# Two products of a high weight joined into one 496-column product: a 4-layer fp32 trunk on one core

## What is computed

```
x += 1/2 * post(SwiGLU_1(pre(x)))         # d_ff = 2816
x += post(Mixer_i(pre(x)))                # layer 0: attention | gated short conv; layer 1: RG-LRU block
x += 1/2 * post(SwiGLU_2(pre(x)))
x += (p[i] @ W_pe) * sigmoid(rmsnorm(x) @ W_pg)
def rmsnorm(x, g): return x * rsqrt(mean(x * x) + EPS) * g
def swiglu(x, wi, wo): g, u = split(x @ wi); return (silu(g) * u) @ wo
```

## Time and profile before

| | |
|---|---|
| median of three runs | 2090.8 us |
| span of the profiled execution | 2089.9 us |
| products and weight loads in it | 17092 each |
| PE busy | 2068.6 us (99%) |
| DVE busy | 1125.9 us (54%) |
| ACT busy | 702.9 us (34%) |
| DMA, mean | 97 GB/s |

### The profile page before, as it was taken

How to read it: one execution, slowest core, us unless ns; L and a number is a source line. 1 busy time by engine, 2 the same in 40 slices (tenths; PEclk the granted TensorE clock), 3 DMA queues, 4 the chain that set the end, 5 groups by cost and what they waited for, 6 DMA issues and landing times.

```text
span 2089.9 us, 37944 instructions
## 1 busy us (share of the span) xinstructions
PE 2068.6 (99%) x17092; PEld 2046.3 (98%) x17092; DVE 1125.9 (54%) x1509; ACT 702.9 (34%) x877; POOL 47.7 (2%) x95
## 2 busy tenths in 40 slices
PE   8999999999999999999999999999999999999999
PEld 8999999999999999999999999999998999999998
DVE  6443244866768543244686342344898854323467
ACT  5221123423354322122444222122487432212243
POOL 0000000022200000000000000000000000000000
PEclk9999999999999999999999999999999999999999
DMA  5222222145321322222222222222222222222222
GB/s 175 90 90 89 96 102 81 62 153 162 127 108 61 122 81 92 91 102 92 101 82 101 82 96 89 99 84 79 86 97 84 82 101 102 89 94 85 98 92 82
DMA packets 35106, 202.79 MB, mean 97 GB/s; under 512 B 5088, under 2 KB 5376, under 8 KB 17024
## 3 DMA queue, kind: packets, MB, share of 16 engines
q1 hardware_dynamic: 29520, 183.87, 25.0%
q0 software_dynamic: 5424, 16.50, 2.5%
HBM read 193.78 MB, written 4.48 MB: 95 GB/s over the span
## 4 chain that ended last, share of the span: by engine, by line
PE 86%; DVE 11%; ACT 2%; issue 1%; DMA 1%; DVEq 0%; ACTq 0%
PE acc L1825 70%; PE acc L1935 10%; DVE w_lo L1120 2%; DVE t L1233 2%; PE acc L1866 1%; DVE x L1240 1%; DVE act_lo L1246 1%; DMA raw<-in_weights 1%; DVE rs_post L1228 1%; PE acc L2015 1%; PE acc L2069 1%; DVE xsum L1255 1%; DVE rs_pre L1228 0%; PE acc L2093 0%; PE acc L2142 0%
## 5 line engine op out<-in xcount | busy, mean ns | idle before, releaser
L1825 PE MATMUL acc<-act_hi,w_hi 128*128 128x260 f32 x3072 | 621.5, 284 | 0.0
L1825 PE MATMUL acc<-act_hi,w_lo 128*128 128x260 f32 x3072 | 617.8, 283 | 0.0
L1825 PE MATMUL acc<-act_lo,w_hi 128*128 128x260 f32 x3072 | 617.4, 282 | 0.0
L1825 PEld LDWEIGHTS acc<-act_hi,w_hi 128*128 128x128 f32 x3072 | 472.4, 188 | 2.7 <-issue 2.0
L1825 PEld LDWEIGHTS acc<-act_hi,w_lo 128*128 128x128 f32 x3072 | 472.6, 188 | 0.4
L1825 PEld LDWEIGHTS acc<-act_lo,w_hi 128*128 128x128 f32 x3072 | 471.8, 188 | 0.5
L723 ACT ACTIVATE w_hi<-raw 128x2048 fp32r<-128x2048 f32 (+3 forms) x179 | 323.0, 1805 | 297.4 <-DMA raw<-in_weights 297.3
L1120 DVE TENSOR_TENSOR w_lo<-raw,w_hi 128x2048 fp32r<-128x2048 f32 (+3 forms) x179 | 386.4, 2158 | 31.7 <-ACT w_hi L723 31.7
L1370 DVE TENSOR_TENSOR gu<-acc,rs_pre 128x520 f32<-128x520 f32 x164 | 114.3, 698 | 441.1 <-PE acc L1825 441.0
L849 ACT ACTIVATE hid_hi<-gu 128x520 fp32r<-128x520 f32 x86 | 55.0, 639 | 476.6 <-DVE gu L1390 476.6
L1825 PE MATMUL acc<-hid_hi,w_hi 128*128 128x260 f32 x1024 | 206.4, 283 | 0.2
(11 more groups left out here) (308 smaller groups left out, 2141.6 us busy)
## 6 DMA issues: line engine op xcount, KB each, us to landing
raw<-in_weights SPq DMA_DIRECT2D x138, 1024.0 KB, 4.8
raw<-in_weights SPq DMA_DIRECT2D x32, 896.0 KB, 4.5
ring<-in_k_pages POOLq DMA_DIRECT2D x16, 256.0 KB, 3.7
raw<-in_weights SPq DMA_DIRECT2D x12, 256.0 KB, 5.3
x<-in_x SPq DMA_DIRECT2D x8, 260.0 KB, 6.5
out_y<-x SPq DMA_DIRECT2D x8, 260.0 KB, 2.1
ckb<-ch_rows POOLq DMA_DIRECT2D x8, 256.0 KB, 4.5
ring<-in_v_pages POOLq DMA_DIRECT2D x8, 256.0 KB, 3.8
```

Source lines behind the costliest of these rows:

```text
L1825: ins = nc.tensor.matmul(a[0:width, half, 0:HALF], w[slot][:, at:at + width], m[:, half * HALF:(half + 1) * HALF], start=first and n == 0, ...
```

## The change

The 520 tokens are cut at 248 instead of 260: the first part has 248 tokens, the second 272. The low and the high part of each split operand lie in one array (`act[:, 0]` low, `act[:, 1]` high), so that the first 248 tokens of both can be read by one product as two runs of 248. A high weight then takes both in one product of 496 columns, whose two runs of results land at two places of one bank, and VectorE adds the two places when it drains. The low weight's product of 248 columns adds to one of the two. The second part (272 tokens) is computed as before. The gates, the recurrent block's `xr`, `gt` and gate tiles, the forget column `f`, the `pe` tiles and the first tiles of layers (`PLAIN`) keep the three products for each half, of 248 and 272 columns.

```diff
-HALF = TOK // 2
+CUT = 248
+TOKENS = (slice(0, CUT), slice(CUT, TOK))
+WIDTH = (CUT, TOK - CUT)
+BANK = 512
...
+PLAIN = {f"{s}.{tile}0" for s in range(0, SUBS, 4) for tile in "gu"} | {"0.g1", f"{S_AB}.f"} | \
+        {f"{s}.pe{m}" for s in range(3, SUBS, 4) for m in range(KC)} | {f"{S_C}.{kind}{m}" for kind, m in C_TILES}
...
-        act_hi = sb("act_hi", [P, KC, TOK], F32R)
-        act_lo = sb("act_lo", [P, KC, TOK], F32R)
+        act = sb("act", [P, 2, KC, TOK], F32R)
+        act_lo, act_hi = act[:, 0, :, :], act[:, 1, :, :]
...
+        def out_half(a, half, parts=P):
+
+            return a[0:parts, 0, BANK - CUT:BANK] if half == 0 else a[0:parts, 1, 0:TOK - CUT]
+
+        def out_parts(a):
+
+            return a[:, :, :].rearrange("p a n -> p (a n)")[:, 0:2 * (BANK - CUT)]                .rearrange("p (r n) -> p r n", r=2)[:, :, 0:CUT]
+
+        def pair_parts(a, m):
+
+            return a[:, m, 0:2 * CUT].rearrange("p (r n) -> p r n", r=2)
...
+            def copy_joined(out, name):
+
+                a = acc_of(name)
+                chained(nc.vector.tensor_copy(cols(out, 1), out_half(a, 1)))
+                drains(nc.vector.tensor_reduce(cols(out, 0), added_parts(a), AXX, ALU.add), name)
...
@@ first_drain
+                if half == 0:
+                    chained(nc.vector.tensor_reduce(out, both_parts(acc_of(name)), AXX, ALU.add))
+                    src = out
...
@@ scaled
-                drains(nc.vector.tensor_tensor(two(out), tile_of(J[name]), two(rs_pre[:, :]), ALU.mult), name)
...
+                a = acc_of(name)
+                ordered(nc.vector.tensor_reduce(cols(out, 0), added_parts(a), AXX, ALU.add))
+                chained(nc.vector.tensor_tensor(cols(out, 1), out_half(a, 1), cols(rs_pre, 1), ALU.mult))
+                drains(nc.vector.tensor_tensor(cols(out, 0), cols(out, 0), cols(rs_pre, 0), ALU.mult), name)
...
@@ out_pair
+                if IS_FFN(s):
+                    if half == 0:
+                        chained(nc.vector.tensor_tensor(out, acc_of(name)[:, :, 0:CUT], out, ALU.add))
+                    ins = nc.vector.tensor_tensor(out, pair_of(J[name], half), out, ALU.add)
+                elif half == 0:
+                    ins = nc.vector.tensor_reduce(out, both_parts(acc_of(name)), AXX, ALU.add)
...
+            def wide_chunk(a, slot, at, split, first, last):
+
+                hi, lo = split[:, 1, :], split[:, 0, :]
+                high, low = w_hi[slot][:, at:at + P], w_lo[slot][:, at:at + P]
+                nc.tensor.matmul(out_parts(a), high, half_of(split, 0), start=first, stop=False)
+                nc.tensor.matmul(out_half(a, 1), high, cols(hi, 1), start=first, stop=False)
+                nc.tensor.matmul(out_half(a, 1), high, cols(lo, 1), start=False, stop=False)
+                nc.tensor.matmul(out_half(a, 0), low, cols(hi, 0), start=False, stop=last)
+                return nc.tensor.matmul(out_half(a, 1), low, cols(hi, 1), start=False, stop=last)
...
@@ half_pair, half 0
+                    if c:
+                        products(w_lo, hi, one_half)
+                    if wait_lo is not None:
+                        wait_lo(c)
+                    ins = products(w_hi, half_of(split, 0), lambda n: pair_parts(accs, n), start=c == 0, stop=c == KC - 1)
+                    if c == 0:
+                        products(w_lo, hi, one_half)
```

More of the change, by code:

```diff
@@ L736, in statistics @@
                 wait_job(act, name)
-                drains(nc.scalar.activation(two(rs[:, :]), tile_of(J[name]), ACT.Sqrt, bias=eps[:, 0:1]), name)
+                drains(nc.scalar.activation(rs[:, :], tile_of(J[name]), ACT.Sqrt, bias=eps[:, 0:1]), name)
             def high(s, c):
@@ L1424, in outputs @@
                     wait_job(dve, name)
-                    out = two(y[:, m, :])
-                    drains(nc.vector.tensor_tensor(out, tile_of(J[name]), out, ALU.add) if IS_FFN(s) else
-                           nc.vector.tensor_copy(out, tile_of(J[name])), name)
+                    out = y[:, m, :]
+                    if IS_FFN(s):
+                        add_joined(out, name)
+                    else:
+                        copy_joined(out, name)
                     done(name)
@@ L2008, in mixer_out @@
                 wait_unit(n)
-                def halves(i, w, part, start, stop):
-                    c = chunks[i]
-                    for m in range(2):
-                        for half in range(2):
-                            ins = nc.tensor.matmul(accs[m][:, half, 0:HALF], w[n % SLOTS][:, (2 * c + m) * P:][:, 0:P],
-                                                   cols(part, half), start=start, stop=stop)
-                        if stop:
-                            ins.then_inc(acc_ready, 1)
@@ new lines, in third @@
+                def third(i):
+                    split = inp(chunks[i])
+                    if i == 0:
+                        accs.append(claim(J[f"{s}.{LAST_PAIRS[0]}.0"]))
+                        wait_unit(n + 1)
+                    for m in range(2):
+                        nc.tensor.matmul(pair_parts(accs[2], m), weight(w_hi, n + 1, i, m), half_of(split, 0),
+                                         start=i == 0, stop=False)
+                    for m in range(2):
+                        ins = nc.tensor.matmul(pair_out(accs[2], 0)[:, m, :], weight(w_lo, n + 1, i, m),
+                                               cols(split[:, 1, :], 0), start=False, stop=i == KC - 1)
+                    if i == KC - 1:
```

218 lines of the change are left out of this document (135 added, 83 removed).

## The result

The changed kernel takes **2130.3 us** (median of 4 runs, 2129.0 to 2134.0) against 2090.5 (2090.0 to 2092.8): ratio 1.0193, 95% interval 1.0179 to 1.0208. It is slower by 39.9 us. The forecast was 2067 with a range of 2038 to 2106, and 0.24 for slower: wrong in sign and outside the range. The profiled execution has a span of 2128.1 us.

What follows compares the result with a forecast made beforehand. The prediction took PE, busy 99% of the span, as the bound: -52.6 (merged products) + 20.3 + 3.6 + 3.8 + 1.0 (waits) = -23.9 us on 2089.9, so 2066.0; median 0.9 above: 2067 us, range 2038 to 2106.

Steps and rivals of the forecast that it cites:

- the price of the 496: Merged product on PE: 209.0 ns for 496 columns, each merge worth 20.5 ns, 2568 merges 52.6 us.
- the mean's row: Profile row of the mean's fp32 products on PE: 520 columns' worth in 219 ns, only 2.3 ns beside them.
- by columns: Rival on PE: excess grows with columns, a 496 costs 228.4 ns, PE gains nothing; +21.2 us, 2112; chance 0.10.
- the 11.4 ns beside the columns: PE: part of a 260-column product's 119.7 ns that is not columns, taken as paid per short product.
- Scaling, joining and low parts: Work on halves of 248 and 272 columns instead of 260: claimed to cancel between the halves.
- Place 1: First pairs of the next sub-layer: PE waits 3.4 us longer for DVE at each of six changes, +20.3 us.
- My sign: Check at the six sub-layer changes: PE's wait for the low part in `first0.1` should be 3 to 5 us each.
- Place 2: Ahead of `post0`: drain of `out67.0` longer by 0.65 us in four sub-layers, 0.49 in two mixers; +3.6 us.
- Place 3: Last chunk of `out0` in the four SwiGLUs: it waits for the up tile's longer drain, +3.8 us.
- Attention: Attention sub-layer: one wait on the drain of an x tile grows, +1.0 us; bounds 0 and 9.8.
- unseen waits: Nearest forecast case, "the unseen": dearer 248-column products or reductions half as dear again, could pass 2112; chance 0.04.

Runs made afterwards that it cites:

- m1: TensorE alone, rows of 48 products of several types and widths: 496 columns take 224.5 ns in fp32r, 209.2 in bf16.
- e1: Changed kernel with every drain as before the change, one instruction on one place, the sum with the other place left out: 2093.1 us, ratio 1.0012.
- e3: Changed kernel with each 496 undone into two 248s adding up in one place and drains as before, leaving only the 248/272 cut: 2100.6 us, ratio 1.0045.
- e4: Changed kernel with the addition of the two places left out only in `first_drain`: 2112.2 us, ratio to before 1.0103.
- e5: Changed kernel with the addition left out only in the drains of output tiles and pairs: 2125.0 us, ratio to before 1.0162.
- e6: Changed kernel with the addition left out only in `scaled`, the drains of the first products' whole tiles: 2116.5 us, ratio to before 1.0126.
- e8: Kernel before, with the low weights' product of `chunk` reading the upper 16 bits of both operands in place as bf16: 2105.4 us, ratio 1.0066.
- e9: Kernel before, with both low products of `chunk` reading the upper 16 bits of their operands in place as bf16: 2090.4 us, ratio 0.9997.
- m2: TensorE alone, bf16 operands read as upper halves of fp32r numbers: both so 115.9 ns at 260 columns, with the moving operand packed 110.8.

## Why the prediction was wrong

- **The step that failed is the price of the 496: "I take 209.0 for the 496, because the mean's row is the nearest in length and has weights of full width."** The nearest in length was of another type. fp32 passes and fp32r ones do not cost the same per column (m1: 0.417 against 0.459 ns), so the earlier trace rows could not show that a long stream hides what a short one doesn't. It measured 225 to 227, which is the case "by columns" (228.4), to which I gave 0.10. Its term was to be -52.6 us; merge and cut together are +2.2 (e1), namely -7.5 for the merge (e3 less e1) and +9.7 for the cut (e3). Of the 11.4 ns beside the columns, which I had put on every short product whatever its length, some 3 are paid per product; the rest grows with the columns.
- **The cut's cost was missing.** I had written: "Scaling, joining and low parts of 248 and 272 columns instead of 260 cancel between the halves": not in the half that is waited for. In e3 PE's chunk with unequal halves is 2.4 ns longer (6.6 us), and the rest of the 9.7 lies mostly in the stretches where DVE works on half 1, now 12 columns wider, and PE waits.
- **Place 1 held in mechanism; that its size came out is luck**: +20.3 was said; the stretch grew by 20.5 in the profile, of which 1.5 are the clock's and some 3 the cut's (e1, without any addition, still has +2.7); e4's median gives 18.1 for the drains. Of the 3.4 us each that I had put, 1.07 were PE's earlier arrival with the 209, which the true chunks hardly bring. And PE waits twice there: for the low parts, as said, and 1.2 us before that for the accumulator, a wait that I had not looked for. My sign, 3 to 5 us of wait for the low part at each change, came out at 1.9 (11.1 over six), and only with the accumulator's 1.2 at 3. How much each is worth by itself was not tried; e4 takes away the cause of both.
- **Place 2 was seen, but not what hangs on the same drains.** +3.6 was said for the wait at `post0`; for all of the output drains e5 gives 5.4 by its median, 9.3 by the stretches of its trace outside of the clock's falls. Most of the rest is the late split of the next pair's weights: drain, ACT's square, ACT's `w_hi`, DVE's `w_lo`, PE. I had followed `out67.0` forward to the mean, and not `out1` forward to the weights. This kind of wait had no row in the trace of before, since it had just enough slack.
- **Place 3 held**: 3.8 said; the four SwiGLUs give back 3.0 in e6. The wait in PE's timeline (0.82 for the product, 1.03 for its load) is of the size that was named:

```profile
349.25 0.49 PE L1919 MATMUL acc<-hid,w_hi 128*128 128x496 f32 x1 [0.82 <-DVE hid L1469]
```

- **Attention was mis-sized**: 1.0 was taken, 0 and 9.8 the bounds; 6.6 us came back in e6. The three-part drain is waited for in front of the scores above all: four times, up to 1.9 us, 4.0 in all, where the kernel before has the one wait of 0.9. Of the other waits of 0.6 to 0.7 us in this body, which the kernel before has not, e6 keeps one. The bounds held, the value taken was at the wrong end.
- Put together, by medians: 18.1 + 5.4 + 13.8 + 2.2 = 39.5 of 39.9 us. By columns I had priced +21.2 (with a slip: at those prices PE comes 0.10 us sooner at place 1, not later, so 6 x 2.4 = 14.5 in place of 13.3, and +22.4 in all); the 18 us between that and the result are the cut (9.7 less 7.5 for the merge, which that case put at nothing), 9 in `scaled`, 5 at place 1 and 2 in the output drains.

The range ended at 2106. To get to 2130 it took the rival "by columns" and unseen waits at once, and I had weighed each by itself.

## What to carry to other kernels

Take a matmul's price from a row of its own type. A row of another type is no bound (0.417 against 0.459 ns a column here), and if no row varies the width of this one, the case of a price per column deserves an even chance. Before merging products on the engine that bounds, price what the merge gives back to the others: here 444 added instructions of a "free" engine at 62% cost 37 us, since DVE is on the path at every change of stage. A drain that gets longer must be followed forward to everything queued behind it on its engine and on the engine that it releases, also where the trace of before shows no wait.

## What the runs showed of the hardware

- In m1, fp32r products: 0.459 ns a column and a floor of 111.6 ns with weights 128 wide; fp32 (both passes counted) and bf16: 0.417 ns a column and 2.5 ns a product; bf16 at 128 columns takes 55.8 ns, so no such floor is seen down to there.
- Going from fp32r to bf16 and back costs some 14 ns a chunk (e8, e9), 13 of them behind the first bf16 product. A strided 16-bit moving operand costs 5 ns in 260 columns, strided weights at most 1 (m2).
- PE's granted clock fell to half behind waits of 0.6 to 2.2 us in some executions and not in others; the one fall in attention in the kernel before (at 523.1, some 3 us) has no wait over 0.3 us in the 12 us ahead of it. Windows of e4 in attention, and of the changed kernel at the same place (from:to, us, PE busy and count, granted clock, DMA share, GB/s):

```profile
457.00:463.00 6.00, 5.27 (x40) 0.92 0.01 4
463.00:466.00 3.00, 3.00 (x15) 0.50 0.00 0
466.00:472.00 6.00, 6.00 (x25) 0.50 0.49 173
472.00:478.00 6.00, 6.00 (x43) 0.97 0.46 179
```

```profile
457.00:463.00 6.00, 4.69 (x33) 1.00 0.00 1
463.00:466.00 3.00, 3.00 (x27) 1.00 0.02 5
466.00:472.00 6.00, 6.00 (x45) 1.00 0.43 131
```

Both had the same two waits there, 0.57 and 0.73 us long (in e4 until 455.0 and 458.9, in the changed kernel until 457.9 and 461.8); the one execution fell to the 1.2 GHz level for some 10 us and lost 5, the other stayed at 2.4 GHz. Of the six changes of sub-layer, each with a wait of 1.6 us, one in the changed kernel's profiled execution and two in e5's had such a fall, of some 3 us and 1.5 lost. Executions of the same kernel lie up to 6 us apart, and in the changed kernel, e4 and e5 the slowest is the one with the lowest granted clock; e4's profiled run (0.996) lies 5 us above its median, the other three (1.000) within 2.
